# Small vectors at the start of a three-block model: the first norm's gain alone, the others through GpSimd's queue

## The reference

```python
def rms_norm(x, g):
    xf = x.astype(jnp.float32)
    y = xf * lax.rsqrt(jnp.mean(xf * xf, axis=-1, keepdims=True) + EPS)
    return (y * g.astype(jnp.float32)).astype(x.dtype)

def swiglu(x, w_gu, w_down):
    gate, up = jnp.split(x @ w_gu, 2, axis=-1)
    return (jax.nn.silu(gate) * up) @ w_down

def first_block(...):
    mem_n = rms_norm(mem, mem_norm)
    ...
    x = x + 0.5 * swiglu(rms_norm(x, ffn1_norm[l]), ffn1_w_gu[l], ffn1_w_down[l])
    h = rms_norm(x, mix_norm[l]) @ a_w_in[i]
    ...
```

## Time and profile before

| | |
|---|---|
| median of three runs | 3026.22 us (3021.07 to 3027.94) |
| the profiled execution | 3027.38 us, of which the instructions span 3025.5 us |
| PE busy | 2878.8 us, 95% |
| PEld busy | 2673.7 us, 88% |
| DVE busy | 1803.6 us, 60% |
| ACT busy | 1477.2 us, 49% |
| POOL busy | 16.3 us, 1% (21 instructions, none of them a DMA) |
| mean granted clock of TensorE | 0.975 |
| DMA | 489.16 MB, 162 GB/s |

### The profile page before, as it was taken

The page is one execution under the profiler, slowest core; times in us unless marked ns, Lnnn a source line. Parts: engine busy times, 40 slices in busy tenths (PEclk is TensorE's granted clock), DMA queues, the critical chain, the costliest instruction groups (busy, mean ns, idle before and its releaser), DMA issues. The chain is left out here.

```text
span 3025.5 us, 47569 instructions
## 1 busy us (share of the span) xinstructions
PE 2878.8 (95%) x20590; PEld 2673.7 (88%) x20590; DVE 1803.6 (60%) x2454; ACT 1477.2 (49%) x1966; POOL 16.3 (1%) x21
## 2 busy tenths in 40 slices
PE   6998898999999999999999999999999999999999
PEld 6997786999997899898999898989999899998898
DVE  4555654656566655546468756455555655656655
ACT  5445423545544544444566544335454544544543
POOL 0000000000000000000000100000000000000000
PEclk9999896999999999999999999999999999999999
DMA  5554211564653355565555255555565456554563
GB/s 196 186 182 140 70 32 46 189 191 153 191 188 114 123 191 181 181 192 170 155 174 161 84 173 172 186 180 168 182 192 169 152 183 194 177 187 154 188 194 127
DMA packets 370037, 489.16 MB, mean 162 GB/s; under 512 B 15183, under 2 KB 329124, under 8 KB 369700
## 3 DMA queue, kind: packets, MB, share of 16 engines
q1 hardware_dynamic: 368944, 485.90, 50.5%
q10 hardware_dynamic: 884, 0.21, 0.0%
HBM read 485.02 MB, written 1.05 MB: 161 GB/s over the span
## 5 line engine op out<-in xcount | busy, mean ns | idle before, releaser
L850 PE MATMUL work<-input_hi,weights_hi 128*128 128x256 f32 x3520 | 991.6, 282 | 8.4 <-DVE weights_lo L232 6.2
L853 PE MATMUL work<-input_hi,weights_lo 128*128 128x256 f32 x3520 | 987.5, 281 | 0.0
L852 PE MATMUL work<-input_lo,weights_hi 128*128 128x256 f32 x3520 | 987.4, 281 | 0.0
L227 DVE TENSOR_TENSOR weights_lo<-weights_raw,weights_hi 128x2048 fp32r<-128x2048 f32 (+2 forms) x282 | 629.6, 2236 | 406.6 <-ACT weights_hi L210 406.4
L850 PEld LDWEIGHTS work<-input_hi,weights_hi 128*128 128x128 f32 x3520 | 666.9, 189 | 13.9 <-DVE weights_lo L232 6.6
L852 PEld LDWEIGHTS work<-input_lo,weights_hi 128*128 128x128 f32 x3520 | 666.7, 189 | 4.4
L853 PEld LDWEIGHTS work<-input_hi,weights_lo 128*128 128x128 f32 x3520 | 666.5, 189 | 0.0
L214 ACT ACTIVATE weights_hi<-weights_raw,params 128x512 fp32r<-128x512 f32 (+2 forms) x736 | 461.9, 701 | 357.7 <-DMA weights_raw<-in_ffn_w_gu 182.2
L210 ACT ACTIVATE weights_hi<-weights_raw 128x2048 fp32r<-128x2048 f32 (+2 forms) x282 | 524.1, 1864 | 178.1 <-DMA weights_raw<-in_ffn_w_up 108.0
L232 DVE SCALAR_TENSOR_TENSOR weights_lo<-weights_raw,params,weights_hi 128x512 fp32r<-128x512 f32 (+2 forms) x736 | 492.7, 733 | 182.8 <-ACT weights_hi L214 182.6
L317 PE MATMUL acc<-weights_hi,hidden_hi 128*128 128x512 f32 x880 | 350.9, 399 | 11.0 <-DVE hidden_lo L953 8.6
(11 more groups left out here) (528 smaller groups left out, 3413.9 us busy)
## 6 DMA issues: line engine op xcount, KB each, us to landing
weights_raw<-in_ffn_w_gu SPq DMA_DIRECT2D x176, 512.0 KB, 4.8
weights_raw<-in_ffn_w_in SPq DMA_DIRECT2D x176, 512.0 KB, 4.8
weights_raw<-in_ffn_w_down SPq DMA_DIRECT2D x66, 1024.0 KB, 4.9
weights_raw<-in_w_in SPq DMA_DIRECT2D x44, 1024.0 KB, 5.3
weights_raw<-in_ffn_w_out SPq DMA_DIRECT2D x44, 1024.0 KB, 4.9
weights_raw<-in_a_w_in SPq DMA_DIRECT2D x29, 1024.0 KB, 5.4
weights_raw<-in_ffn_w_gate SPq DMA_DIRECT2D x44, 512.0 KB, 4.0
weights_raw<-in_ffn_w_up SPq DMA_DIRECT2D x44, 512.0 KB, 5.0
```

The lines of the kernel that those rows point to most:

```text
L227: last = self.nc.vector.tensor_tensor(self.wl[:, n % SLOTS, 0:kc * cols], raw, self.wh[:, n % SLOTS, 0:kc * cols].bitcast(F32), ALU.subtract)
L850: nc.tensor.matmul(o, wh[:, k, ms], K.hi[:, c, :], start=(c == 0 and m == 0), stop=False, skip_group_check=True)
L852: nc.tensor.matmul(o, wh[:, k, ms], K.lo[:, c, :], start=False, stop=False, skip_group_check=True)
L853: last = nc.tensor.matmul(o, wl[:, k, ms], K.hi[:, c, :], start=False, stop=(c == DC - 1), skip_group_check=True)
```

## The change

`ffn1_norm` moves to the front of the list of vectors and so to partitions 0 to 15 of the first tile. Its one DMA (16 x 128) is all that ScalarE's queue issues; it counts on the same semaphore as the identity. TensorE waits for both, transposes these 16 rows first of all, and VectorE copies 16 columns into `params` before it splits the quarters of `x`.

The other 19 DMAs are issued by GpSimd's queue, behind its own clearing of the tile. Their transposes move into `MemoryKeys.project`, which TensorE runs behind step 0 of the first layer, into bank 1 of `acc`; the copy of the other 496 columns moves into `MemoryKeys.scale` on VectorE. `sum_squares` (TensorE), `root_and_round` (ScalarE) and `normalise` (VectorE) now also wait for that copy. `turned` is counted one higher in `root_and_round`.

```diff
--- before.py
+++ after.py
@@ -696,14 +696,16 @@
 def start(K, feed):
     nc, A = K.nc, K.A
     rows = K.ctx2.enter_context(K.fresh("vector_rows", [P, 4, P], F32))
+    K.vector_rows = rows
     cleared, turned, copied = (K.count_of(s) for s in ("rows_cleared", "transposed", "copied"))
     first_constants, vectors_loaded = K.count_of("identity_loaded"), K.count_of("vectors_loaded")
     x_loaded = [K.count_of(f"x_tile_{t}_loaded") for t in range(NT)]
     vectors = [("mem_norm", A["mem_norm"]), ("kv_in", A["kv_in_norm"]), ("kvlat", A["kv_lat_norm"]), ("bq", A["b_q_norm"][0]),
                ("aout", A["a_out_norm"][0]), ("conv_b", A["conv_b_2"]), ("ssm_norm", A["ssm_norm_w_2"]),
                ("b_gate", A["b_gate_2"]), ("v_gain", A["a_v_norm_3"][0]), ("pool_scale", A["b_scale_3"][0])]
-    groups = [([name], v.rearrange("(c p) -> c p", p=P)) for name, v in vectors]
-    for names, v in ((["ffn1_0", "ffn1_1"], A["ffn1_norm"]), (["mix_0", "mix_1"], A["mix_norm"]),
+    groups = [(["ffn1_0", "ffn1_1"], A["ffn1_norm"].rearrange("n (c p) -> (n c) p", p=P))]
+    groups += [([name], v.rearrange("(c p) -> c p", p=P)) for name, v in vectors]
+    for names, v in ((["mix_0", "mix_1"], A["mix_norm"]),
                      (["ffn2_0", "ffn2_1"], A["ffn2_norm"]), (["mix3_0", "mix3_1"], A["mix_norm_3"]),
                      (["ffn3_00", "ffn3_01", "ffn3_10", "ffn3_11"], A["ffn_norm_3"].rearrange("a b d -> (a b) d")),
                      ([f"conv_a{k}" for k in range(4)], A["a_conv"][0]), ([f"conv_s{k}" for k in range(4)], A["conv_w_2"])):
@@ -720,6 +722,8 @@
             done += k
         at += n
     assert at <= 4 * P
+    _, _, urgent, urgent_src = pieces.pop(0)
+    K.first_params = urgent
 
     split_at = CONSTS["tri64"][0]
     with K.stage(join=True) as (block, _):
@@ -728,6 +732,9 @@
         @block.gpsimd
         def _(pool):
             nc.gpsimd.memset(rows[:, :, :], 0.0).then_inc(*cleared.up())
+            pool.wait_ge(*cleared(1))
+            for tile, p, k, src in pieces:
+                nc.gpsimd.dma_start(rows[p:p + k, tile, :], src).then_inc(*vectors_loaded.up(16))
 
         @block.sync
         def _(sp):
@@ -743,8 +750,7 @@
         @block.scalar
         def _(act):
             act.wait_ge(*cleared(1))
-            for tile, p, k, src in pieces:
-                act.dma_start(rows[p:p + k, tile, :], src).then_inc(*vectors_loaded.up(16))
+            act.dma_start(rows[0:urgent, 0, :], urgent_src).then_inc(*first_constants.up(16))
             for i in range(4):
                 feed.round_quarter(act, i)
             act.wait_ge(*copied(1))
@@ -754,20 +760,17 @@
 
         @block.tensor
         def _(pe):
-            pe.wait_ge(*first_constants(16))
+            pe.wait_ge(*first_constants(32))
+            nc.tensor.transpose(K.acc[:, 0, 0:urgent], rows[0:urgent, 0, :], K.c("ident")[0:urgent, 0:urgent]).then_inc(*turned.up())
             for i in range(4):
                 feed.turn(pe, i)
-            pe.wait_ge(*vectors_loaded(16 * len(pieces)))
-            for tile in range(4):
-                last = nc.tensor.transpose(K.acc[:, 0, tile * P:(tile + 1) * P], rows[:, tile, :], K.c("ident"))
-            last.then_inc(*turned.up())
 
         @block.vector
         def _(dve):
+            dve.wait_ge(*turned(1))
+            nc.vector.tensor_copy(K.params[:, 0:urgent], K.acc[:, 0, 0:urgent]).then_inc(*copied.up())
             for i in range(4):
                 feed.split_quarter(dve, i)
-            dve.wait_ge(*turned(1))
-            nc.vector.tensor_copy(K.params[:, :], K.acc[:, 0, :]).then_inc(*copied.up())
             dve.wait_ge(*copied(1))
             K.split_weights(dve, 2)
             feed.invert_root(dve)
@@ -1786,15 +1789,21 @@
         self.squared, self.rooted, self.inverse, self.normed = (
             K.count_of("norm_" + s) for s in ("squared", "rooted", "inverse", "normed"))
         self.rounded, self.split = K.count_of("source_rounded"), K.count_of("source_split")
+        self.vectors_loaded, self.vectors_copied = K.count_of("vectors_loaded"), K.count_of("copied")
 
     def sync_part(self, sp):
         sp.dma_start(self.mem[:, :, :], self.K.A["mem"][0].rearrange("(t p) d -> p t d", p=P)).then_inc(*self.loaded.up(16))
 
     def project(self, pe, n):
-        pass
+        K = self.K
+        pe.wait_ge(*self.vectors_loaded(0))
+        for tile in range(4):
+            last = K.nc.tensor.transpose(K.acc[:, 1, tile * P:(tile + 1) * P], K.vector_rows[:, tile, :], K.c("ident"))
+        last.then_inc(*self.turned.up())
 
     def sum_squares(self, pe):
         K = self.K
+        pe.wait_ge(*self.vectors_copied(1))
         for j in range(4):
             t, half = j // 2, j % 2
             pe.wait_ge(*self.normed(t + 1))
@@ -1831,7 +1840,9 @@
             .then_inc(*self.rooted.up())
 
     def scale(self, dve):
-        nc, col = self.K.nc, self.col
+        K, nc, col = self.K, self.K.nc, self.col
+        dve.wait_ge(*self.turned(1))
+        nc.vector.tensor_copy(K.params[:, K.first_params:], K.acc[:, 1, K.first_params:]).then_inc(*self.vectors_copied.up())
         dve.wait_ge(*self.rooted(1))
         nc.vector.reciprocal(col[:, 2, :], col[:, 1, :]).then_inc(*self.inverse.up())
         dve.wait_ge(*self.inverse(1))
@@ -1844,9 +1855,10 @@
 
     def root_and_round(self, act):
         K = self.K
+        act.wait_ge(*self.vectors_copied(1))
         for j in range(4):
             t, half = j // 2, j % 2
-            act.wait_ge(*self.turned(j + 1))
+            act.wait_ge(*self.turned(j + 2))
             for c in range(4):
                 at = 4 * half + c
                 last = K.nc.scalar.activation(self.hi[:, at, t * P:(t + 1) * P], K.acc[:, j, c * P:(c + 1) * P], ACT.Copy,
@@ -1855,6 +1867,7 @@
 
     def normalise(self, dve):
         K = self.K
+        dve.wait_ge(*self.vectors_copied(1))
         for j in range(4):
             t, half = j // 2, j % 2
             dve.wait_ge(*self.rounded(j + 1))
```

## The result

Four runs of the changed kernel took 3003.72 to 3007.82 us, median 3005.75; four of the kernel before on the same occasion 3021.07 to 3027.94, median 3024.14. The ratio is 0.9939, with a 95% interval of 0.9921 to 0.9956: 18.4 us faster, 13 to 24 us by the interval. The forecast was 3014 us and a range of 3010 to 3022, so the direction was right, and the size and the range were not. Two more comparisons, on other occasions, gave 0.9958 (0.9944 to 0.9972) and 0.9940 (0.9927 to 0.9952). All 15 runs of the changed kernel have a mean of 3005.1 us (standard error 0.6), all 59 of before one of 3020.3 us (0.5): the best value for the gain is 15.2 us, give or take 1.6 (two standard errors). The first comparison's 18.4 us lean on four runs of before whose mean, 3024.3 us, is 4.0 us above that of the 59. Whether that is chance or the occasion, the runs do not tell.

The account below looks back on a forecast made before the run. Two serial delays before the first weights product, ScalarE's issuing and the slowest small vector, were taken as the bound; the rest only shifts. 3026.2 (median of three) - 12.4 = 3013.8, about 3014 us; range 3010 to 3022 us.

Parts of the forecast that it names:

- ScalarE's queue and the urgent row: At the start: ScalarE free at 1.9 us, the row landed at 4 to 5 us; term bounded at 0 to 2 us.
- The quarters of `x` and the weights: ScalarE starts on item 0 at 10.6 instead of 23.06 us, 12.4 us earlier; first product at 16.1 us.
- What the shift meets: Transfers already on their way, item 4 and `mem`, still land in time, with 2.9 and 3.7 us to spare.
- TensorE behind step 0 and VectorE: The four moved transposes (0.6 us) and the 496-column copy (0.69 us) fit into idle time and cost nothing.
- GpSimd's queue: 19 issues of 1.15 us each from 1.3 us: issued by 23.2 us, vectors landed by 31.4 at the longest tail.
- The bound of 31.7 us: Latest time for all vectors to land without loss: TensorE reaches their transposes at 29.1 us, 2.6 us of stall free.
- rivals B and C: GpSimd's issues cost about 2 us each, 3025 to 3031 us (0.12); or 2.5 us each, about 3036 us (0.05).
- Rival A: VectorE's splits of weights hold GpSimd up, vectors land at about 38 us, 6.3 us lost: 3020 us (0.12).
- Rival D: Urgent row or items 0 and 1 land late, 1 to 3 us lost: 3015 to 3017 us; 0.68 together with the forecast.
- The shift itself: TensorE never idles from 100 us on, so an earlier first product ends the whole program that much earlier, 12.4 us.
- GpSimd's stall: TensorE waiting at L1801 for late vectors: 6.3 us in rival A, 11 to 17 us in rival B.
- theory 2: From the experiments: the changed program itself is faster in the mixers, the column order in `params` for one.

Follow-up runs that it names:

- split only: The changed kernel with ScalarE's queue issuing all 20 small DMAs, the first norm's rows first, urgent/late split kept; 3013.55 us, ratio 0.9979 to before.
- GpSimd late: The changed kernel with GpSimd's 19 issues held back until ScalarE has rounded item 2; 3008.89 us, ratio 0.9965 to before.
- delay of 5: The changed kernel with 5 extra ScalarE activations between its last rounding of x and first rounding of weights; 3012.08 us, ratio 0.9971 to before.
- GpSimd's queue only: The kernel before with all 20 small DMAs issued by GpSimd's queue, transposes and copy still ahead of the first weights; 3015.11 us, ratio 0.9982.
- delay of 11: The changed kernel with 11 extra ScalarE activations between its last rounding of x and first rounding of weights; 3016.92 us, ratio 0.9990 to before.
- both fillings: The changed kernel with 36 extra TensorE transposes behind the turning of x and 20 behind item 2; 2998.51 us, ratio 0.9941 to before.
- the one at the start: The changed kernel with only 36 extra TensorE transposes behind the turning of x; 3002.94 us, ratio 0.9941 to before.
- the late one: The changed kernel with only 20 extra TensorE transposes behind item 2, ahead of the memory's transposes; 2999.70 us, ratio 0.9925 to before.

## Why the prediction was right and where it failed

- *ScalarE's queue and the urgent row*: right. The row landed at 4.97 us, forecast 4 to 5; split only shows that the queue alone keeps ScalarE until 12.9 us.
- *The quarters of `x` and the weights*: right to 0.4 us. The rounding of item 0 starts at 10.27 us, the first product at 15.71. The next bound is item 1's landing, 0.44 us of waiting where 0.2 us of spare had been worked out.
- *What the shift meets*: right for the transfers. Not in the sum: that the slow matmuls behind TensorE's idle time would be more (24 instead of 13, 1.1 us), and the slow stretch behind the second idle time longer. Of 12.8 us 11.0 to 12.3 are left at the end of the layer, 11.5 in the mean, where 12.4 had been put down.
- *TensorE behind step 0 and VectorE*: right. L1801 without a wait, 0.60 us, inside the idle time; the copy took 0.67 us of VectorE's 3 us.
- *GpSimd's queue*: the mechanism was right and the size off by half: 0.49 to 0.67 us an issue, 0.51 in the mean, where 1.15 was taken, and 4.7 to 5.5 us from each issue to its landing, so that the vectors had landed by about 16.3 us instead of 31.4. The bound of 31.7 us was never near, and rivals B and C did not come. The reason given for twice ScalarE's mean, that a descriptor made by software should cost more, was not borne out: ScalarE's own mean of 0.58 us was the nearest row. That mean and the worst case of 2.09 us each rest on a pair of issues of which one took 0.27 and the other 3.88 us. The tail was taken from the same queue, where it is 8.3 us; on GpSimd's it is 4.3 to 4.8.
- *Rival A*: fell by GpSimd late. *Rival D*: 0.44 us of waiting came, and the first product was still earlier than forecast.
- *The step that failed* is the sum: "less 12.4 it is 3015.0", "so that the forecast is 3026.2 - 12.4". Its first term, 3026.2 us, was the median of three runs; 59 runs of the same kernel have a mean of 3020.3 us, 5.9 us lower. Its second term, 12.4 us for the start, measured 11.5. And it has no term for anything behind the start, where 3.7 us more were gained. From 3013.8 us these three lead to the mean of 3005.1 that was measured: -5.9, +0.9 and -3.7. With a base of 3020.3 the same sum gives 3007.9 us.
- *Why the base could be so far off*: the prediction says of TensorE's idle time "From 100 us on it does not: in the window of 100 to 200 us it is busy for 100.00 of 100 us. What happens at the start is therefore a shift". The window of 100 to 200 us is a feed-forward layer. In the mixers behind it TensorE idles, its granted clock falls to 0.50, and how long that lasts is not the same in every execution: the first mixer took 301.8 to 311.1 us in 13 executions of kernels whose code is equal there. The three runs of before had shown 6.9 us of scatter, and the prediction put 0.03 on more than that. 59 runs show 15.3 us, with a standard deviation of 4.0. A range of 12 us around one time was too narrow by that, and more than half of it was spent on the side of GpSimd's stall. The shift itself, that what the start gains arrives at the end, is borne out by delay of 5, GpSimd's queue only and split only within two standard errors of their means.
- *What stays open*: the cause of the 3.7 us that remain between the means, beyond the start. By the same reckoning (gain in the means, less what the one profiled execution shows at the eleventh product) delay of 5 has 0.5 us of them (7.9 and 7.3), GpSimd's queue only 0.5 (5.0 and 4.5), split only 2.1 (6.0 and 3.9), delay of 11 about 3 (2.8 and -0.2), GpSimd late 2.1, both fillings 3.8, the one at the start 2.8 and the late one 10.0, each with an error of 1 to 2 us. No one cause that was tried orders their sizes. But all kernels with the split, save delay of 5, have 2 us or more, and the one that only moves the queue has next to none, which is what theory 2 would look like. It was seen only afterwards, delay of 5 speaks against it, and no experiment separates the split from the order of the columns in `params` that came with it.

## What to carry to other kernels

Look at what the first useful product waits for, and split what is loaded for it from what is loaded for later: here two serial delays, a queue that the rounding engine had to serve and one slow small transfer, hid behind one wait, and taking away either alone was worth 5 of 12.8 us. When a window shows an engine 100% busy, check every kind of stage behind it before saying that all the rest only shifts; where TensorE idles in a stage, the clock there is a term with a scatter of its own. For a change of 0.5%, take more than three runs of the kernel before, for the base of the forecast too, look at the granted clock beside each time, and compare one fixed pair of instructions in both timelines instead of two totals.

## What the runs showed of the hardware

- GpSimd's queue issues a small DMA in 0.48 to 0.67 us whatever its rows (1 to 107), and each landed 4.7 to 5.5 us behind its issue in the changed kernel (3.2 to 5.5 in GpSimd late). ScalarE's queue took 0.27 to 0.59 us, for the 107 rows too (0.27), but 3.88 us for the DMA behind those, of 21 rows (3.93 in split only). VectorE's splits L232 beside GpSimd's issues made no difference.
- The tail behind the last issue was 8.3 us from ScalarE's queue and 4.8 and 4.3 us from GpSimd's, for the same rows beside much the same transfers.
- Behind some 6 us without work TensorE's first 13 to 24 matmuls of 128x256 took 0.41 us instead of 0.28 while the granted clock read 1.00; 36 transposes in the idle time took that away. In three executions of the same program the stretch behind a shorter idle time of 2.8 to 2.9 us ran twice at a granted clock of 0.50 and once at 1.00.
- The times of one program go with its mean granted clock: 2.2 us for every 0.001, over 55 runs of about 3020 us.
- The first mixer's time was the same to 0.2 us in two executions of before, and to 0.1 us in two of three of the changed kernel (1.7 us less in the third), and yet differed by up to 9 us between kernels whose code is equal there.
